# A hybrid decoder layer on eight cores: seventeen block turns move from TensorE to transposing DMAs

## The reference

```python
h = rmsnorm(x, norm_mix)
u, gb, gc, v = split(h @ w_in)                   # 4 x 512 channels
d = trailing_mean(u, window=2/4/8/16 by group) - u
a = (d @ w_pool) * pool_scale
b = gb * causal_dwconv3(gc * v, conv_w)
x = x + concat(a, b) @ w_out
h = rmsnorm(x, norm_ffn)
up = causal_dwconv3(h @ w_up, ffn_conv_w) + ffn_conv_b      # 2 x 2816 channels
x = x + (silu(gate) * val) @ w_down
y = rmsnorm(x, norm_final)
```

## Time and profile before

| | |
|---|---|
| runs of the kernel | 727.80, 728.96, 747.03 us; median 728.96 |
| the profiled execution | 728.0 us, span of its slowest core 726.4 us |
| spans of the other cores | 720.1 to 725.9 us |
| mean granted TensorE clock | 0.977 to 0.985 of full speed |
| PE / DVE / ACT / POOL busy | 95% / 68% / 48% / 30% of the span |
| stretch of stage 3 of tile 1 | about 288 to 370 us |
| hand-overs (`window0`, `window(1)`, `window(2)`) | 225 to 288, 398 to 449, 555 to 606 us |

### The profile page before, as it was taken

The page is one execution under the profiler, slowest core; times in us unless marked ns, Lnnn a source line. Parts: engine busy times, 40 slices in busy tenths (PEclk is TensorE's granted clock), DMA queues, the critical chain, the costliest instruction groups (busy, mean ns, idle before and its releaser), DMA issues.

```text
span 726.4 us, 12730 instructions; the slowest of 8 cores (720.1 to 726.4 us)
## 1 busy us (share of the span) xinstructions
PE 689.3 (95%) x3788; PEld 334.7 (46%) x3788; DVE 492.2 (68%) x846; ACT 347.0 (48%) x809; POOL 215.5 (30%) x414
## 2 busy tenths in 40 slices
PE   5869799889999999999999999999999999999996
PEld 4534345445554454444444444444444444444442
DVE  4277767578886245788878566877777276888724
ACT  4344342567775112877643233766621234666521
POOL 2242100467774000455431000444420001443300
PEclk8989899989999999999999999999999999999999
DMA  8998593887787456999989430999987212980002
GB/s 198 234 170 125 97 214 62 131 146 132 126 137 152 67 164 166 172 189 187 184 150 164 145 117 1 177 166 163 155 144 123 105 71 54 162 135 1 4 29 88
DMA packets 26742, 94.62 MB, mean 130 GB/s; under 512 B 3358, under 2 KB 3742, under 8 KB 26674
## 3 DMA queue, kind: packets, MB, share of 16 engines
q0 software_dynamic: 18288, 66.59, 56.5%
q1 hardware_dynamic: 8242, 26.95, 11.1%
q10 hardware_dynamic: 144, 0.26, 0.1%
HBM read 150.36 MB, written 10.01 MB: 221 GB/s over the span
## 4 chain that ended last, share of the span: by engine, by line
PE 82%; DMA 7%; DVE 5%; issue 2%; ACT 2%; DVEq 0%; SPq 0%; ACTq 0%; POOL 0%; POOLq 0%
PE G L598 53%; PE G L905 12%; PE G L906 12%; DMA wslot<-w_str 3%; DMA yp<-x1b 3%; PE TR L598 2%; PE TR L554 2%; PE G L1142 1%; DMA x1b<-xp 1%; DVE w_down_sb L769 1%; DVE arena L769 1%; ACT hbuf L496 0%; DVE arena L830 0%; DVE arena L842 0%; DVE actT L558 0%
## 5 line engine op out<-in xcount | busy, mean ns | idle before, releaser
L969 ACT ACTIVATE arena<-G,cst_sb 128x512 f32<-128x512 f32 x176 | 135.4, 776 | 86.2 <-PE G L598 85.1
L598 PE MATMUL G<-aT,wslot 128*128 128x512 bf16 x736 | 165.8, 383 | 1.3 <-DVE arena L1007 1.0
L998 DVE SCALAR_TENSOR_TENSOR arena<-G,cst_sb,arena 128x512 f32<-128x512 f32 x176 | 124.0, 747 | 43.7 <-ACT Esave L974 41.0
L598 PE MATMUL G<-aT,sm_arena 128*128 128x512 bf16 x672 | 146.8, 379 | 0.0
L1007 DVE SCALAR_TENSOR_TENSOR arena<-G,cst_sb,arena 128x512 f32<-128x512 f32 x176 | 125.5, 744 | 4.9 <-DVE OFp L1005 0.5
L905 PE MATMUL G<-w_down_sb,actT 128*128 128x512 bf16 x330 | 125.1, 379 | 0.0
L906 PE MATMUL G<-w_down_sb,actT 128*128 128x512 bf16 x330 | 125.1, 379 | 0.0
L978 POOL TENSOR_TENSOR actT<-arena 128x512 bf16<-128x512 f32 x88 | 95.5, 1086 | 72.9 <-ACT arena L976 60.9
L598 PEld LDWEIGHTS G<-aT,wslot 128*128 128x128 bf16 x736 | 71.3, 99 | 85.3 <-issue 4.9
L598 PEld LDWEIGHTS G<-aT,sm_arena 128*128 128x128 bf16 x672 | 65.7, 98 | 78.6
L496 ACT ACTIVATE hbuf<-x1b 128x1024 bf16<-128x1024 f32 x29 | 30.7, 1057 | 136.5 <-DVE x1b L868 110.8
(11 more groups left out here) (167 smaller groups left out, 775.2 us busy)
## 6 DMA issues: line engine op xcount, KB each, us to landing
wslot<-w_str POOLq DMA_DIRECT2D x58, 512.0 KB, 7.3
sm_arena<-w_str POOLq DMA_DIRECT2D x50, 512.0 KB, 7.4
x1b<-xp SPq DMA_DIRECT2D x13, 512.0 KB, 5.0
yp<-x1b SPq DMA_DIRECT2D x12, 512.0 KB, 3.9
w_down_sb<-w_down POOLq DMA_DIRECT2D x11, 512.0 KB, 10.3
xrot<-xp SPq DMA_DIRECT2D x10, 512.0 KB, 6.3
w_down_sb<-w_str POOLq DMA_DIRECT2D x4, 512.0 KB, 18.9
w_out_sb<-w_out POOLq DMA_DIRECT2D x4, 512.0 KB, 15.0
```

What stands on the lines that cost most here:

```text
L598: ins = e.matmul(out_ap, lhsT=wslot[slot][:, k, half * 128:(half + 1) * 128], rhs=rhsT[:, k, c0:c0 + ncols], start=(k == 0), stop=(k == nk ...
L969: P.op("act", lambda e, tp=tp, g=g, c=c, h=h: e.activation(out=tp[:, h, 2:514], in_=G[g][:, :], func=AF.Identity, scale=cc(C_FW + 3 * c), ...
L998: P.op("dve", lambda e, g=g, c=c, h=h: e.scalar_tensor_tensor(out=tp[:, h, 1:513], in0=G[g][:, :], scalar=cc(C_FW + 3 * c + 1), in1=tp[:, ...
```

## The change

`norm_transpose` gets a flag `dma`. Where it is set, the norm has three steps: `scale` as before; `turn_dma`, one transposing DMA from SP that writes the turned `hbuf` straight to its place in `hT` or `aT`; and `weigh`, the multiply with the norm's weight, in place on DVE in SBUF, after which the `hbuf` is free. The flag is set for norm 1 of tiles 2 and 3 (8 blocks) and for norm 2 of blocks 0 to 2 of tiles 1 to 3 (9 blocks). The hand-overs are written anew so that `turn_dma` directly follows `scale` and `weigh` comes later, and the table `N1_AT` gives the DMA step three and the multiply six steps after the start of its block.

```diff
-        def norm_transpose(src, nrows, srckeys, hb, hk, dstT, col0, gcol, dstkeys, power=False, act_scale=False):
+        def norm_transpose(src, nrows, srckeys, hb, hk, dstT, col0, gcol, dstkeys, power=False, act_scale=False, dma=False):
...
+            def turn_dma():
+                P.op("sp", lambda e: e.dma_start_transpose(out=dstT[:, :, col0:col0 + 128], in_=hb[:, :]), reads=[hk],
+                     writes=dstkeys, dsem=f"D_turn{HKI[hk]}")
+
+            def weigh():
+                dst = dstT[:, :, col0:col0 + 128]
+                P.op("dve", lambda e: e.tensor_tensor(
+                    out=dst, in0=dst, in1=cst_sb[:, gcol:gcol + 8].unsqueeze(2).to_broadcast([128, 8, 128]), op=ALU.mult),
+                    reads=["cst"], writes=dstkeys)
+                hfree.append(HKI[hk])
+            if dma:
+                return Steps(scale, turn_dma, weigh)
...
-            return norm_transpose(src, 128, sk, hb, hk, dst, i * 128, C_G1, keys(i), power, act_scale)
+            return norm_transpose(src, 128, sk, hb, hk, dst, i * 128, C_G1, keys(i), power, act_scale, dma=(s >= 2))
...
-            return norm_transpose(x1[r], 128, [("x1", r)], hb, hk, aT, i * 128, C_G2, [("aT", k, i) for k in range(8)])
+            return norm_transpose(x1[r], 128, [("x1", r)], hb, hk, aT, i * 128, C_G2, [("aT", k, i) for k in range(8)],
+                                  dma=(s >= 1 and i < 3))
...
+        def s2_tail(s, n2):
+            for i in range(len(n2), 4):
                 n2.append(s2_block(s + 1, i))
-                if i == 0:
-                    pb.pop(0)()
-                if i >= 1:
+                if i >= 2 and n2[i - 2].fns:
+                    n2[i - 2].step()
+                if i >= 1 and n2[i - 1].fns:
                     n2[i - 1].step()
-                if i >= 2:
-                    n2[i - 2].step()
+                    n2[i - 1].step()
             gab = (galloc(), galloc())
             s4_mm(3, ALLK[0:8], True, False, gab)
             n2[3].step()
...
+            n1_two(0)
+            if nx2 is not None:
+                load_xrot(nx2, 2)
+                load_xrot(nx2, 3)
+            load_x1(s + 1, 0)
+            for i in range(3):
+                s4_block(s, i)()()
+                load_x1(s + 1, i + 1)
+                if i == 1:
+                    n1_weigh(0)
+                    n1_two(2)
+            n1_weigh(2)
+            return s2_tail(s, [])
...
-            for fn, dj in ((n1_start, 0), (n1_scale, 2), (n1_turn, 4)):
+            for fn, dj in ((n1_start, 0), (n1_scale, 2), (n1_turn, 3), (n1_turn, 6)):
```

More of the change, by code:

```diff
@@ L1218, in window, with n1_two, n1_weigh @@
             return lambda: s4_post(s, 3, gab)()
+        def window(s):
+            nx2 = s + 2 if s + 2 < NST else None
+            pb = []
+            def n1_two(i):
+                if nx2 is None:
+                    return
+                for n in (i, i + 1):
+                    pb.append(norm1_block(nx2, n))
+                for n in (i, i + 1):
+                    pb[n].step()
+                for n in (i, i + 1):
+                    pb[n].step()
+            def n1_weigh(i):
+                for p in pb[i:i + 2]:
+                    p.step()
+            n1_two(0)
[11 more added lines that the diff above has]
+            return s2_tail(s, [])
         def window0():
@@ L1228, in window0 @@
                 if i == 0:
+                    n2[0].step()
                     n2[0].step()
@@ L1240, in window0 @@
             pump()
[L1241 to L1246, removed]
+            post3 = s2_tail(0, n2)
             load_xrot(2, 0)
             load_xrot(2, 1)
[L1249 to L1256, removed]
+            return post3
         def sample_state_outputs_s1():
```

## The result

| | |
|---|---|
| runs of the changed kernel | 752.09, 754.41, 754.51, 773.38 us; median 754.46 |
| against the kernel before, on the same chip | ratio 1.0355, 95% interval 1.0335 to 1.0375: slower |
| its profiled execution | 754.5 us, span of the slowest core (5) 753.0 us |
| spans of cores 0 to 7 | 745.6, 746.9, 734.0, 751.6, 731.3, 753.0, 727.8, 741.7 us |
| predicted | 745 us, range 722 to 778 |

Some executions of every kernel here are some per cent longer, with a lower granted clock on some cores, whatever the kernel (773.38 and 747.03 in the tables are such): ratios, times and comparisons leave these executions out or, where no other was left, their disturbed cores.

What follows compares the result with a forecast made beforehand. It took PE, busy 689.3 of 726.4 us, as the bound. From 728.0 us it subtracted 7.65 for removed turns, added 19.3 of hand-over stalls and 5.4 for the clock: +17.0, 745 us, range 722 to 778.

Steps and rivals of the forecast that it cites:

- Norm 1 inside the up projection of tile 1: Four turns there, multiply three weight steps (10.3 us) after its turn; cost taken as 0 for L up to 10.
- L: Time from end of scaling on DVE until the weight's multiply may start; taken as 5 us, ends 2.3 and 10.3.
- Rival C: Tile 1's up projection: multiplies come too early, four transfers each 3 us late, up to +12 us; 0.07 with something unseen.
- 3L - 6.4: PE's stall in us at the end of tile 2's hand-over, three transfers in series on DVE; 8.6 us forecast.
- 3L - 7.8: PE's stall in us at the end of tile 3's hand-over, three transfers in series; 7.2 us forecast.
- rival A: Hand-overs: transfers are quick, L about 2.3 to 3.3, total 720.8 to 724.8 us; chance 0.20.
- Rival B: A block's eight squares turned one after another, L about 7 to 12; 788 us at L = 10; chance 0.15.
- L - 2.4: PE's stall in us in tile 1's hand-over for L up to 4.1, 2L - 6.5 beyond; 3.5 us forecast.
- The clock: Lower PE clock after long stalls: 2.7 us each in tiles 2 and 3, 5.4 in all; nothing for tile 1.
- 0.45 us for each turn: PE time saved by each of the 17 turns removed, 7.65 us in all.
- the in-place multiply: On DVE, SBUF to SBUF in place of the PSUM read: 1.13 us between starts, so 0, at worst 1 us.
- 0 for the four turns of norm 1 in the hand-over: Hand-over from tile 1 to 2: cover of a down-projection block (9.9 us) or some 8 us, so no cost.

Runs made afterwards that it cites:

- experiment 2: Kernel before, with only the four norm-1 turns inside tile 1's up projection by DMA: 753.36 and 753.53 us, +24.5.
- experiment 3: As experiment 2, but each turn a plain copy of the same 256 KB to a spare buffer in 2 KB rows: 727.09 us (one run).
- experiment 4: As experiment 3, but the plain copy goes to the turns' own place in hT in 256-byte runs, not turned: 750.63 us (one run).
- experiment 12: Changed kernel without the four norm-weight multiplies in tile 1's up projection, all 17 turns still by DMA: 778.1 and 779.6 us.
- version 7: As version 6, with each multiply behind the next block's scale on DVE: 725.48 and 725.28 us; in five rounds ratio 0.9934 to the kernel before.
- experiment 1: Changed kernel with the four turns of tile 1's up projection back on PE, 13 left by DMA: 735.45 us, ratio 1.0087 to the kernel before.
- version 6: As experiment 1, with tile 1's two 512 KB input loads issued at the start of the hand-over: 730.08 us, kernel before 729.79.
- experiment 11: Version 7 with the last two of tile 1's hand-over turns back on PE, 11 by DMA: ratio 0.9932 to the kernel before.

## Why the prediction was off

**The step that failed is "Norm 1 inside the up projection of tile 1", priced at 0** with a cover of 10.3 us. It cost 8.8 + 12.7 idle and 4.5 by the clock on core 5, and 24.5 us by itself in experiment 2. I priced the transfers by bytes: 256 KB beside an input load of 512 KB that needs 10.0 us, so less than 10. A load of that size has 144 packets, a turn 1,056, and turns landed in 26 and 40 us, the second held behind the first. That the destination is written in runs of 128 tokens, 256 bytes, stands in the diff; I used this ("a transpose has to scatter every row") only to argue about L in the hand-overs, where it hardly mattered. Experiments 3 and 4, same bytes and 144 against 1,040 packets, 727 and 751 us, show that this was the main missing term. The cover itself was not short of the 10.3 us: DVE reached the first multiply at 324.4 us, 14.4 after the turn's issue.

**Rival C named this place and this wait** (DVE's multiply, PSUM behind it), and I gave it 3 us for each of four turns, with something unseen a chance of 0.07. Place and wait were right in the changed kernel; the price was two turns of 11.8 and 14.7 us, and experiment 12 shows that lateness of the queue is the cause and the multiply only where it shows.

**L was 3.0 us, not 5.** Tiles 2 and 3: the formulas 3L - 6.4 and 3L - 7.8 give 2.6 and 1.2 at L = 3, measured 2.9 and 1.8. The formulas held within 0.6 us, and version 7 shows their cause, the order on DVE: with the scale ahead of the multiply both gaps vanish. Only L was mis-sized: I took it from the middle of loads with other traffic, while the DMA shares of 0.05 and 0.02 said that the low end was right. This is rival A. Rival B's eight squares in series don't happen: all eight are turned within 2.8 us. The Trainium skill's "as fast as regular DMAs" (Advanced Engine Details and Errata, "X-Bar Transpose (TRN2)") agrees roughly with the quiet turn: 2.8 us, between the 2.0 of a store of the same 256 KB and the 3.3 of the input load of 512 KB at 455 us. In the loaded stretch, 30 us beside 10 to 11 for experiment 3's plain copy, it does not hold.

**Tile 1: L - 2.4 would give 0.6**; measured 2.5 us of gap on core 5 of the changed kernel, with 1.7 by the clock, and 5.9 on the slowest core of experiment 1. Step missed: L is no constant. For the last turn it was 5.75 us on core 5 (the formula then gives 3.4) and 7.5 on that slowest core; part of this is two 512 KB loads issued behind the turn (version 6), where I had looked for loads ahead of the turns only.

**The clock**: 5.4 us charged in tiles 2 and 3, where single gaps of at most 1.6 us cost none. It fell where gaps were long, after 12.7 us: 2.85 us for 16 matmuls, near the 2.4 priced; and after tile 1's 2.5 us (1.7 us), to which I had charged nothing.

**What held**: 0.45 us for each turn (experiment 11), the in-place multiply at 1.23 us and no cost of its own, 0 for the four turns of norm 1 in the hand-over. That 745 us came near 754 is luck: an excess of 20 us in the hand-overs (19.3 + 5.4 less the 4.4 of L = 3) stood in for 26 us in a place priced 0; had L alone been right, the sum would have said 724.8, and been further off.

## What to carry to other kernels

Price a transfer by its packets as well as its bytes, and by what shares the DMA engines at that moment: the same turn landed in 2.8 us in a quiet stretch and in up to 51 us beside a weight stream. Move such a transfer only where the DMA share is low, look at what is issued behind it as well as ahead, and put the instruction that waits for it behind everything on its engine that does not. When a wait is removed in a trial and the time gets longer, the wait may be a symptom: look for the queue behind it.

## What the runs showed of the hardware

- A 128x1024 bf16 turn from SBUF to SBUF is 1,056 packets, a plain copy of the same block 144. Alone it lands 2.8 us after issue, at 280 to 300 GB/s while it moves (changed kernel, core 5, 459 to 462 us); SP's issue takes 1.22 us, where that of a plain 512 KB load takes 0.33.
- Beside a weight stream SP's issue of a turn can be held 18 to 24 us, nearly until the turn ahead of it lands (experiments 2 and 12); a plain copy in 256-byte packets held it for 1.7 us at most (experiment 4, cores 0, 3 and 6). The input loads between the turns land in a median of 28.2 us (300 to 420 us of experiment 12, core 0), where they needed 10.0.
- Beside transposing packets what the DMA engines move can fall at a share of 1.0 and more (84, 112 and 117 GB/s in three of the four ten-us stretches from 320 to 360 us of core 5, 203 in the other; 175 to 198 in the kernel before). Only the 84 falls wholly into a time in which PE ran and called for weights. A full share is no sign of many bytes.
- Plain 256-byte packets delay only their own queue (weights at 10.0 us), transposing ones the weights too (19.4).
